# Router work of two MoE layers moved from behind the out projections to between their tiles

## The chip, the cores and the metric

One core of one Trainium2 chip runs the whole kernel. The metric is the device time of one launch in microseconds (us), median of the runs.

## The reference, cut to what matters

Two layers over 512 latent tokens and 256 context tokens of width 1024 (8 blocks of 128). In each layer a mixer writes `y`, and then a routed mixture of 16 experts follows. What the change touches:

```python
def modulate(x, g, shift, scale):
    return rms_norm(x, g) * (1 + scale) + shift
...
h = h + mod_l[2] * y_lat                       # out projection, gate, residual
h = h + mod_l[5] * expert_choice_ffn(modulate(h, ln2_g[layer], mod_l[3], mod_l[4]), *moe)
...
def expert_choice_ffn(h, w_router, w_gate, w_up, w_down):
    cap = max(1, EC_CAPACITY * t // N_EXPERTS)
    aff = jax.nn.softmax((h @ w_router).astype(F32), axis=-1)
    gate, idx = lax.top_k(jnp.swapaxes(aff, 1, 2), cap)
    xs = jax.vmap(lambda hb, ib: hb[ib])(h, idx)
    hid = jax.nn.silu(xs @ w_gate) * (xs @ w_up)
```

`cap` is 64 tokens of the latents and 32 of the context for each expert. Layer 0 routes both streams, layer 1 the latents alone.

## The kernel before, in words

Tokens lie in 6 tiles of 128 rows: tiles 0 and 1 are context, 2 to 5 latents. H holds the residual stream, one tile per 1024 columns. Each engine runs one written program, in order; an engine that waits on a semaphore runs nothing that stands behind the wait. There is no planner.

**Out projection.** Layer 0: `outproj0_pe` (L1781), tiles in the order YORDER = [0, 1, 4, 3, 5, 2], two halves of 512 columns each, so 12 halves j = 0 to 11. A half is 8 float32 products of 128x128 by 512 columns (L1789; the profile counts two records for a product). The first four halves have had 4 of their 8 products earlier. Layer 1: `outproj_pe` (L1812), 4 latent tiles, 8 halves (L1821). For each half DVE (`outproj_dve`, L1828) multiplies the result by the gate (L1838) and adds the half before it to H (L1846). PE may run four halves ahead (`op_ok`).

**Norm and router.** After the last half, ACT squares and sums each tile (L351; all but the last tile lie beside the projection), takes one root for all (L355), DVE inverts it (L371) and writes the normalised rows XM, tile by tile (L378). PE turns XM (L403: 48 transposes in layer 0, 32 in layer 1), DVE and ACT apply scale and shift per channel while copying out of PSUM to AM (L390, L364), and PE multiplies AM by the router weight in two parts (`logits_pe`, L1912; four blocks of channels side by side in 32-column groups). The four partial sums are copied (L1964, L1947), turned back (L1929) and added (L1974) into AFF. Then `pick_dve` (L1960): softmax from L1975 on, and the top tokens by eight rounds of max, index and replace (L1993 to L1996).

**Token lists and first pair.** The picks are turned (L1940), and DVE writes the lists TOKF, TOKL, TOKC, TOKX, TOKH (L2017 to L2031) and raises one semaphore, `sg`, at the last. POOL (`moe_pool`, L2323) then gathers rows of XM from memory: 128 latent rows for a pair of experts (L2328) and, in layer 0, 64 context rows (L2330); both raise `got`. PE waits for both, turns them (L2138, L2142) into banks 0, 1 and 4; DVE scales and shifts (L2244, 8 instructions, `xs` at the eighth), ACT the context rows (L2218, `xsc`). `pair` (L2167) waits for both and starts the expert products (L2104 latents, L2114 context).

**Queues.** SP's queue in `rows_sync` (L2043) stores H tiles (layer 0) as they are ready, issues seven 1 MB loads of expert rows after the first tile (`first_rows`, L2369), after the projection the rest of the first 8 (layer 1: 12) loads, and then stores all XM tiles. Later loads are released by PE slot by slot (L2367, `x_free`). POOL's queue loads the latents back to H (L2872, 2 MB), and in layer 0 the router weight WR only when the projection has ended (L2875, 64 KB); in layer 1 FING (L2879) and then WR (L2880) after the first half.

Of the kernel before, what the change touches and what calls it, by code (L numbers as in the profile page):

```python
# [12 lines left out]
P = 128  # L13
D = 1024
# [128 lines left out]
def build(nc, t, out):  # L143

    ctx = ExitStack()
    with ctx:
# [70 lines left out]
        dve_step, pool_step = sem("dve_step"), sem("pool_step")  # L217
# [104 lines left out]
        NORMS = ["n1_0", "n2_0", "n1_1", "n2_1"]  # L322
# [45 lines left out]
        def norm_dve(dve, n, tiles, xn, w, A, by_column=False, between=None, ready=None):  # L368
            runs, tiles0, ctx0 = before(n)
            dve.wait_ge(rt_ok, runs + 1)  # L370
            nc.vector.reciprocal(stat_t[:, 16 + tiles[0]:16 + NT], stat_t[:, 8 + tiles[0]:8 + NT]).then_inc(rc_ok, 1)  # L371
            dve.wait_ge(rc_ok, runs + 1)
            if n in ROUTED:
                nc.vector.memset(LG.rearrange("p t e -> p (t e)"), 0.0)
# [18 lines left out]
        def norm_pe(pe, n, tiles, xn, ctx_too):  # L393
            runs, tiles0, ctx0 = before(n)
            pe.wait_ge(xn_ok, tiles0 + len(tiles))
            for k in range(KT):
# [8 lines left out]
                if k == 5 and n in ROUTED:  # L405
                    logits_pe(pe, int(n[-1]), 0)
# [58 lines left out]
        for k in range(KT):  # L465
# [4 lines left out]
        g_mm, g_act, g_diff, g_ek, g_tr, g_rowT, g_rows = (sem(n) for n in (  # L470
            "g_mm", "g_act", "g_diff", "g_ek", "g_tr", "g_rowT", "g_rows"))
# [93 lines left out]
        def gates_rows_dve(dve):  # L565
            dve.wait_ge(g_tr, 1)
            nc.vector.tensor_copy(ROWT[0:32, 0:512], ps[0:32, 5, :])
            nc.vector.tensor_copy(ROWT[0:32, 512:768], ps[0:32, 6, 0:256]).then_inc(g_rowT, 1)
# [12 lines left out]
        def gates_exps_act(act):  # L581
# [3 lines left out]
            nc.scalar.activation(EK, GLAST, ACT.Exp).then_inc(g_ek, 1)  # L585
# [12 lines left out]
        def gates_rows_pe(pe):  # L598
# [5 lines left out]
            tr.then_inc(g_tr, 1)  # L604
# [223 lines left out]
        def gqa_act(act):  # L828
# [45 lines left out]
        cv_zero, cv_x, cv_c, cv_s, cv_tr, cv_outd, cv_outa, cv_xc = (sem(n) for n in (  # L874
            "cv_zero", "cv_x", "cv_c", "cv_s", "cv_tr", "cv_outd", "cv_outa", "cv_step"))
# [61 lines left out]
        def conv_dve(dve):  # L937
            step = Chain(dve, cv_xc)
# [73 lines left out]
        dn_qk, dn_zero, dn_step = (sem("dn_" + n) for n in "qk zero step".split())  # L1012
# [768 lines left out]
        def outproj0_pe(pe):  # L1781
# [23 lines left out]
            for j in range(2 * NT):  # L1805
                if j < 4:
                    half_products(j, range(4, KT))
                else:
                    pe.wait_ge(op_ok, j - 3)
                    half_products(j, turned + list(range(4, KT)))  # L1810

        def outproj_pe(pe, u0, tiles, ycols, mm_sem, ok_sem, base=0):  # L1812

            for j in range(2 * len(tiles)):
# [10 lines left out]
                if j < 2 * len(tiles) - 1:  # L1825
                    mm.then_inc(mm_sem, 1)

        def outproj_dve(dve, u0, tiles, mm_sem, prod_sem, ok_sem, w, PROD, base=0, banks=(4, 5, 6, 7)):  # L1828
            n = 2 * len(tiles)
            for j in range(n + 1):  # L1830
                if j < n:
                    tt, half = tiles[j // 2], j % 2
                    if j < n - 1:
                        dve.wait_ge(mm_sem, max(base - 1, 0) + j + 1)
                    else:
                        dve.wait_ge(w_free, u0 + KT)
                    v = 1 if tt < CT else 0
                    nc.vector.tensor_tensor(PROD[:, j % 4, :], ps[:, banks[j % 4], :], GATE[:, w, v, half * 512:half * 512 + 512],  # L1838
                                            ALU.mult).then_inc(ok_sem, 1)
                if j >= 1:  # L1840
                    tt, half = tiles[(j - 1) // 2], (j - 1) % 2
                    dve.wait_ge(ok_sem, base + j)
                    if w == 0 and base == 0:
                        dve.wait_ge(h_back if tt < CT else h_late, 16)
                    hh = H[:, tt, half * 512:half * 512 + 512]
                    nc.vector.tensor_tensor(hh, hh, PROD[:, (j - 1) % 4, :], ALU.add).then_inc(prod_sem, 1)  # L1846
# [5 lines left out]
        AM = region(6144, KT * AW, "p (k t) -> p k t", k=KT)  # L1852
# [30 lines left out]
        LT4 = region(13312, TOK, "p (t n) -> p t n", t=NT)  # L1883
        lg_ctx, lg_lat = sem("lg_ctx"), sem("lg_lat")
# [16 lines left out]
        def logits_pe(pe, l, half):  # L1901


            if half == 0:
                pe.wait_ge(mo["wr"], 16 * (l + 1))
            spans = [(4, LO, LAT)] + ([(5, 0, CTX)] if l == 0 else [])
            for bank, first, n in spans:
                for j in range(4):
                    k = 4 * half + j
                    w = WR[:, k, :]  # L1910
                    w = bass.AP(w.tensor, w.offset, [w.ap[0], [1, 32]])
                    mm = pe.matmul(ps[32 * j:32 * j + 32, bank, 0:n], w, AM[:, k, first:first + n],  # L1912
                                   start=(half == 0), stop=(half == 1))
            if half == 1:
                mm.then_inc(mo["lg"], 1)

        def pick_pe(pe, l):

            runs, _, ctx0 = before(NORMS[2 * l + 1])
            pe.wait_ge(am_ok, KT * (runs + 1))  # L1920
            if l == 0:
                pe.wait_ge(ac_ok, ctx0 + KT)
            logits_pe(pe, l, 1)
# [971 lines left out]
```

## Time and profile before

| | us |
|---|---|
| median of 3 runs | 2386.52 (2384.01 to 2393.23) |
| profiled execution, span first to last instruction | 2382.3 |
| PE busy in the span | 2112.3 (89%) |
| DVE busy | 762.8 (32%) |
| ACT busy | 447.2 (19%) |
| POOL busy | 121.9 (5%) |
| first out projection, from the end of its set-up | 749.4 to 818.1 |
| second out projection | 1794.1 to 1849.4 |

The page gives the profiled execution by its span alone; a time of its own around that span is not recorded, so the median stands beside it, 4.2 us longer. Times in the rows are in us from the span's start. L12 is line 12 of the kernel. PE is the matmul engine, DVE the vector engine, ACT the scalar engine, POOL GpSimd, SP the queue engine. PEclk is the granted clock of PE, 1.00 for 2.4 GHz and 0.50 for 1.2 GHz.

### The profile page before, as it was taken

Reading aid. Unit: us, or ns where it says so; the run is one execution under the profiler, and the core shown is the slowest. Engines: PE = TensorE matmul, PEld = TensorE weight load, DVE = VectorE, ACT = ScalarE, POOL = GpSimd, SP = SyncE. Lnnn points to the kernel's source line nnn. Section 1 sums busy time; section 2 is a strip of 40 time slices with the busy share of each in tenths; the row PEclk is TensorE's granted clock in tenths of the full one; section 3 lists DMA queues with packets and bytes.
Section 4 is the critical chain, followed back from the end, with each engine's and each line's share of the span. In section 5 each row is a group of like instructions: output and inputs, shape, how many; then the busy total and the mean of one; then the engine's idle time right before and its main releaser. Section 6 shows DMA issues by size and latency. Waiting matters only on the chain.

```text
span 2382.3 us, 32937 instructions
## 1 busy us (share of the span) xinstructions
PE 2112.3 (89%) x13760; PEld 1076.7 (45%) x13760; DVE 762.8 (32%) x1384; ACT 447.2 (19%) x1008; POOL 121.9 (5%) x119
## 2 busy tenths in 40 slices
PE   5998999818689849999999989999999399999997
PEld 3544666517685413333333334554674144444442
DVE  2143523588874341011011113000681511111113
ACT  2213421575321110000000012000561000000001
POOL 0000000030110000011111000000000000000000
PEclk9999999857679969999999999999999699999999
DMA  7219730132125339999999982210313399999996
GB/s 285 71 64 345 248 130 13 38 95 84 63 77 200 113 126 378 398 395 399 390 398 395 401 343 77 60 44 1 111 41 134 132 408 421 421 421 421 421 421 276
DMA packets 110618, 551.30 MB, mean 231 GB/s; under 512 B 13024, under 2 KB 25824, under 8 KB 61328
## 3 DMA queue, kind: packets, MB, share of 16 engines
q1 hardware_dynamic: 102512, 522.29, 55.6%
q0 software_dynamic: 7168, 23.83, 3.5%
q10 hardware_dynamic: 800, 3.15, 0.3%
q8 instruction: 111, 1.82, 0.3%
q14 instruction: 27, 0.22, 0.0%
HBM read 525.27 MB, written 22.38 MB: 230 GB/s over the span
## 4 chain that ended last, share of the span: by engine, by line
PE 75%; DMA 11%; DVE 9%; ACT 2%; issue 2%; SPq 0%; POOL 0%; DVEq 0%; POOLq 0%; ACTq 0%
PE ps L2104 22%; PE ps L2114 5%; DMA ring_sb<-expert_w_up 5%; PE ps L498 5%; PE ps L1789 3%; PE ps L901 3%; PE ps L2468 3%; PE ps L1821 2%; PE ps L2440 2%; PE ps L2449 2%; PE ps L2132 2%; DMA ring_sb<-ada_w 2%; PE ps L2151 2%; PE ps L900 2%; PE ps L244 2%
## 5 line engine op out<-in xcount | busy, mean ns | idle before, releaser
L2104 PE MATMUL ps<-work_sb 128*32 128x512 f32 (+1 forms) x2432 | 408.1, 593 | 9.6 <-ACT work_sb L2235 5.5
L2104 PE MATMUL ps<-ring_sb,work_sb 128*32 128x512 f32 (+1 forms) x2048 | 300.5, 599 | 16.6 <-DMA ring_sb<-expert_w_up 9.8
L2104 PEld LDWEIGHTS ps<-work_sb 128*32 128x32 f32 (+1 forms) x2432 | 123.0, 120 | 231.5 <-issue 224.2
L2104 PEld LDWEIGHTS ps<-ring_sb,work_sb 128*32 128x32 f32 (+1 forms) x2048 | 87.8, 118 | 204.3 <-issue 198.1
L2291 DVE TENSOR_TENSOR work_sb<-ps,work_sb 128x512 f32<-128x512 f32 x32 | 20.6, 687 | 437.1 <-PE ps L2114 329.8
L2225 ACT ACTIVATE work_sb<-ps 128x1024 f32<-128x1024 f32 x16 | 16.4, 1024 | 515.9 <-PE ps L2114 295.8
L498 PE MATMUL ps<-ring_sb,work_sb 128*128 128x512 f32 (+1 forms) x288 | 109.2, 541 | 0.9 <-DVE work_sb L390 0.9
L2114 PE MATMUL ps<-work_sb 128*32 128x512 f32 x768 | 100.7, 592 | 0.0
L2114 PE MATMUL ps<-ring_sb,work_sb 128*32 128x512 f32 x768 | 100.4, 593 | 0.0
L901 PE MATMUL ps<-work_sb,ring_sb 128*128 128x512 f32 x192 | 98.0, 592 | 0.0
L2310 DVE SCALAR_TENSOR_TENSOR work_sb<-ps,work_sb,gates_sb 128x1024 f32<-128x1024 f32 x16 | 20.5, 1284 | 232.9 <-PE ps L2114 124.8
L2235 ACT COPY work_sb<-ps 128x512 f32<-128x512 f32 x32 | 17.3, 589 | 405.7 <-PE ps L2192 405.7
L244 PE MATMUL ps<-ring_sb,sT_sb 128*32 128x512 f32 x384 | 57.0, 692 | 30.0 <-DMA ring_sb<-ada_w 28.2
L1789 PE MATMUL ps<-ring_sb,work_sb 128*128 128x512 f32 x192 | 82.8, 592 | 0.0
L498 PEld LDWEIGHTS ps<-ring_sb,work_sb 128*128 128x128 f32 x288 | 55.6, 194 | 52.4 <-issue 46.2
L2253 DVE TENSOR_TENSOR h_sb<-ps,h_sb 128x512 f32<-128x512 f32 x64 | 42.5, 688 | 100.2 <-PE ps L2151 100.2
L2468 PE MATMUL ps<-ring_sb,work_sb 128*128 128x512 f32 x160 | 68.8, 592 | 0.0
L2244 DVE TENSOR_SCALAR work_sb<-ps,scaleT_sb,modT_sb 128x128 f32<-128x128 f32 x128 | 42.2, 403 | 82.5 <-PE ps L2132 65.0
L2449 PE MATMUL ps<-work_sb,ring_sb 128*128 128x512 f32 x128 | 65.4, 592 | 0.0
L784 DVE TENSOR_REDUCE work_sb<-ps 128x1 f32<-128x768 f32 (+1 forms) x48 | 35.2, 775 | 78.5 <-PE ps L708 78.5
L2151 PE MATMUL ps<-work_sb 128*128 128x512 f32 x128 | 58.9, 604 | 1.5 <-DVE work_sb L2310 1.5
L2104 PE MATMUL ps<-h_sb,work_sb 128*64 128x512 f32 x128 | 57.6, 592 | 0.6 <-DMA work_sb<-expert_w_down 0.6
(405 smaller groups left out, 2913.2 us busy)
## 6 DMA issues: line engine op xcount, KB each, us to landing
work_sb<-expert_w_down SPq DMA_DIRECT2D x88, 1024.0 KB, 17.4
work_sb<-expert_w_gate SPq DMA_DIRECT2D x64, 1024.0 KB, 9.5
ring_sb<-expert_w_gate SPq DMA_DIRECT2D x64, 1024.0 KB, 10.0
ring_sb<-expert_w_up SPq DMA_DIRECT2D x64, 1024.0 KB, 13.9
work_sb<-expert_w_up SPq DMA_DIRECT2D x56, 1024.0 KB, 14.6
ring_sb<-ada_w SPq DMA_DIRECT2D x96, 512.0 KB, 6.2
ring_sb<-expert_w_down SPq DMA_DIRECT2D x32, 1024.0 KB, 14.4
ring_sb<-wout SPq DMA_DIRECT2D x16, 512.0 KB, 6.5
```

Source lines behind the costliest of these rows:

```text
L244: mm = pe.matmul(ps[32 * q:32 * q + 32, bank, :], sT[:, k, :], w[:, a * 512:(a + 1) * 512], start=(k == 0), stop=(k == KT - 1))
L498: mm = pe.matmul(ps[:, j % 4, 0:N], A[:, k, tok_cols(tt):tok_cols(tt) + P], w[:, (k % 2) * N:(k % 2 + 1) * N], start=(k == 0), stop=(k == ...
L900: pe.matmul(ps[:, b + 1, 0:CTX], w[:, k, :], A[:, k, 0:CTX], start=(k == 0), stop=(k == KT - 1))
L901: mm = pe.matmul(ps[:, b, :], w[:, k, :], A[:, k, LO:LO + LAT], start=(k == 0), stop=(k == KT - 1))
L1789: mm = pe.matmul(ps[:, EVEN_BANKS[j % 4], :], YT[:, tt, k, :], w[:, half * 512:half * 512 + 512], start=(k == 0), stop=(k == KT - 1))
L1821: mm = pe.matmul(ps[:, 4 + j % 4, :], c(k), w[:, half * 512:half * 512 + 512], start=(k == 0), stop=(k == KT - 1))
L2104: mm = pe.matmul(ps[g:g + wide, bank + n, :], lat_src[:, k, g:g + wide], us[e][:, n * 512:(n + 1) * 512], start=(k == 0), stop=(k == KT - 1))
L2114: mm = pe.matmul(ps[g:g + 32, bank_c, :], ctx_src(k, e), us[e][:, n * 512:(n + 1) * 512], start=(k == 0), stop=(k == KT - 1))
L2132: mm = pe.matmul(ps[:, k // 4, k % 4 * P:(k % 4 + 1) * P], XM[:, CT + j, cols(k)], TAKE[:, p % 2, j, :], start=(j == 0), stop=(j == LT - 1))
L2151: pe.matmul(ps[:, 4 + g % 4, :], ONEHOT[:, j * P:(j + 1) * P], YL[l][:, half * 512:half * 512 + 512], start=True, stop=True).then_inc(h_mm, 1)
L2449: mm = pe.matmul(ps[:, b, :], w[:, k, :], AO[:, k, LO:LO + LAT], start=(k == 0), stop=(k == KT - 1))
L2468: mm = pe.matmul(ps[:, 2 * (i % 2) + side, :], AO[:, k, v_cols(m):v_cols(m) + P], w, start=(k == 0), stop=(k == KT - 1))
```

## The change

The separate norm (`n2_0`, `n2_1`) and `logits_pe` go. The raw residual tile H is turned instead of the normalised one. The per-channel scale is multiplied into the router weight (WRM); the shift times the router weight becomes one row per stream (CROW, spread over the partitions as CVEC); the root of the mean square is applied to the logits. All of that is written between the halves of the out projection. PE:

```diff
+    def route_beside_pe(pe, l, j):        # called after the products of half j
+        if j == 1:
+            route_shift_pe(pe, l)         # waits for WR; 8 products, 16 columns
+        if j >= 4 and j % 2 == 0:
+            route_back_pe(pe, l, j // 2 - 2)
+        if j >= 2 and j % 2 == 0:
+            route_turn_pe(pe, l, j // 2 - 1)
+        if j == 3:
+            route_spread_pe(pe, l)
+        if j >= 3 and j % 2 == 1:
+            route_logits_pe(pe, l, (j - 3) // 2)
+    def route_end_pe(pe, l):              # after the last half
+        last = len(routed_tiles(l)) - 1
+        route_back_pe(pe, l, last - 1)
+        route_turn_pe(pe, l, last)
+        route_logits_pe(pe, l, last)
+        route_back_pe(pe, l, last)
+    def route_turn_pe(pe, l, n):
+        tt = routed_tiles(l)[n]
+        pe.wait_ge(op_x, OP0 * l + 2 * n + 2)
+        if n > 0:
+            pe.wait_ge(rt_dve, NT * l + n)
+            pe.wait_ge(rt_act, NT * l + n)
+        for k in range(KT):
+            tr = pe.transpose(ps[:, TURN_BANKS[l][k // 4], k % 4 * P:(k % 4 + 1) * P], H[:, tt, cols(k)], IDENT)
+            if k % 4 == 3:
+                tr.then_inc(rt_mm, 1)
+    def route_logits_pe(pe, l, n):
+        ...
+        for half in range(2):
+            pe.wait_ge((rt_dve, rt_act)[half], NT * l + n + 1)
+            for j in range(4):
+                k = 4 * half + j
+                ...
+                mm = pe.matmul(ps[32 * j:32 * j + 32, LOGIT_BANK[l], 0:P], w, RT[:, k, :], start=(half == 0), stop=(half == 1))
+        mm.then_inc(rl_mm, 1)
+    def route_back_pe(pe, l, n):
+        pe.wait_ge(rl_ok, logits_ok(l, 2 * n + 3))
+        pe.transpose(ps[:, BACK_BANK[l], 0:P], TURNED, IDENT).then_inc(rl_mm, 1)
```

DVE, the new body of `outproj_dve` for each half j, and what it calls:

```diff
+            for j in range(n):
+                ...
+                nc.vector.tensor_tensor(PROD[:, j % 4, :], ps[:, banks[j % 4], :], GATE..., ALU.mult).then_inc(ok_sem, 1)
+                dve.wait_ge(ok_sem, base + j + 1)
+                ...
+                nc.vector.tensor_tensor(hh, hh, PROD[:, j % 4, :], ALU.add).then_inc(prod_sem, 1)
+                if j == 2:
+                    router_weights_dve(dve, l)
+                if j % 2 == 0 and j >= 4:
+                    route_sums_dve(dve, l, j // 2 - 2)
+                if j % 2 == 1 and j >= 5:
+                    route_logits_dve(dve, l, (j - 5) // 2)
+                if j % 2 == 1 and j >= 3:
+                    route_dve(dve, l, (j - 3) // 2)
+            last = len(tiles) - 1
+            route_sums_dve(dve, l, last - 1)
+            route_dve(dve, l, last)
+            route_logits_dve(dve, l, last - 1)
+            route_sums_dve(dve, l, last)
+            route_logits_dve(dve, l, last)
+    def route_dve(dve, l, n):             # half of the turned tile, root, XM
+        ...
+        nc.vector.tensor_copy(RT[:, 0:4, :]..., ps[:, TURN_BANKS[l][0], :]).then_inc(rt_dve, 1)
+        dve.wait_ge(rt_ok, tile_roots_before(l) + n + 1)
+        nc.vector.reciprocal(...).then_inc(rc_ok, 1)
+        dve.wait_ge(rc_ok, tile_roots_before(l) + n + 1)
+        nc.vector.tensor_scalar(XM[:, tt, :], H[:, tt, :], stat_t[:, 16 + tt:17 + tt], None, ALU.mult).then_inc(xn_ok, 1)
+    def route_sums_dve(dve, l, n):
+        ...
+        nc.vector.tensor_copy(TURNED, ps[:, LOGIT_BANK[l], 0:P]).then_inc(rl_ok, 1)
+    def route_logits_dve(dve, l, n):
+        ...
+        nc.vector.tensor_reduce(LG[:, tt, :], groups, AX, ALU.add).then_inc(lg_ok, 1)
+        dve.wait_ge(lg_ok, NT * l + n + 1)
+        nc.vector.scalar_tensor_tensor(AFF[:, tt, :], LG[:, tt, :], ..., CVEC[...], ALU.mult, ALU.add).then_inc(rl_ok, 1)
```

ACT (`route_act`) squares each tile when both halves are in H, copies blocks 4 to 7 of the turned tile to RT (`rt_act`), and takes the root per tile. SP stores XM tile n - 1 behind H tile n and the last before the remaining expert loads. `router_weights_dve` forms WRM, copies CROW, and in layer 0 has the four memsets that stood in `pick_dve`. POOL's queue:

```diff
-            pool.wait_ge(gate_ok, 4)
-            pool.wait_ge(w_free, U_MOE[0])
+            pool.wait_ge(dn_ok, len(ORDER))
             pool.dma_start(WR, t["router"][0]...).then_inc(mo["wr"], 16)
...
             pool.wait_ge(op_mm, OP0)
+            pool.dma_start(WR, t["router"][1]...).then_inc(mo["wr"], 16)
             pool.dma_start(FING, ...).then_inc(fin_in, 16)
-            pool.dma_start(WR, t["router"][1]...).then_inc(mo["wr"], 16)
```

Token lists and first pair: TOKL is written first and raises `sg`, then TOKC raises it again (layer 0), the rest raises `sg_all`. The two gathers have semaphores of their own (`got`, `gotc`), and the latent rows of layer 0 are turned into banks 6 and 7.

```diff
-                pe.wait_ge(mp["got"], 32 * p + 32 if l == 0 else 32 * NPAIR + 16)
+                pe.wait_ge(mp["got"], 16 * (NPAIR * l + p + 1))
...
                 if l == 0:
+                    pe.wait_ge(mp["gotc"], 16 * p + 16)
...
+                    if m == 0 and k % 4 == 0:
+                        pe.wait_ge(mp["xs"], 2 * (NPAIR * l + p) + (k // 4 + 1 if l == 0 else 2))
...
+                        if m == 0 and k == 0:
+                            pe.wait_ge(mp["xsc"], p + 1)      # before the context products of block 0
```

Some semaphores elsewhere are merged (`g_tr` and `g_ek` into others, the convolution's chain into the common one) with the same instructions between them.

## Rows read from the trace of the kernel before

**Rows 1.** The page: chain shares by engine, and the group of the first out projection.

```profile
PE 75%; DMA 11%; DVE 9%; ACT 2%; issue 2%; SPq 0%; POOL 0%; DVEq 0%; POOLq 0%; ACTq 0%
...
L1789 PE MATMUL ps<-ring_sb,work_sb 128*128 128x512 f32 x192 | 82.8, 592 | 0.0
```

**Rows 2.** Chain of waits, in order of time, 720 to 900 us: start, us, what.

```profile
749.37 68.68 PE ps L1789 x160
...
818.69 1.71 DVE h_sb L1846 x2
...
841.20 0.27 DVE work_sb L1975
...
867.59 5.87 DMA work_sb<-xm_rows,work_sb
873.59 1.97 PE ps L2138 x8
875.59 2.65 DVE work_sb L2244 x8
...
879.31 3.64 PE ps L2104 x16
```

**Rows 3.** Chain of waits, 1848 to 1905 us.

```profile
1849.35 0.69 DVE work_sb L1838
...
1867.80 0.23 DVE work_sb L1975
```

**Rows 4.** Timeline of DVE, 720 to 815 us: start, us, engine, line, operation.

```profile
735.51 0.69 DVE L1751 TENSOR_TENSOR h_sb<-h_sb,work_sb 128x512 f32<-128x512 f32 x1
736.24 0.69 DVE L1752 TENSOR_TENSOR h_sb<-h_sb,work_sb 128x512 f32<-128x512 f32 x1
...
756.28 0.69 DVE L1838 TENSOR_TENSOR work_sb<-ps,gates_sb 128x512 f32<-128x512 f32 x1 [2.74 <-PE ps L1789]
756.89 0.68 DVE L1846 TENSOR_TENSOR h_sb<-h_sb,work_sb 128x512 f32<-128x512 f32 x1
```

**Rows 5.** Timeline, 63 us: a copy of 128 columns out of PSUM.

```profile
63.19 0.28 DVE L536 COPY work_sb<-ps 128x128 f32<-128x128 f32 x1
```

**Rows 6.** Timeline of PE: transposes, router logits, and 64-wide products.

```profile
747.46 1.91 PE L1761 MATMUL ps<-base_sb,h_sb 128*128 128x128 f32 x16
...
833.57 1.50 PE L1912 MATMUL ps<-work_sb 128*32 128x512 f32 x16
...
1787.97 1.09 PE L2540 MATMUL ps<-work_sb 128*64 128x128 f32 x16 [0.33 <-ACT work_sb L2621]
```

**Rows 7.** POOL's load of the latents; DMA issues, us to landing, 700 to 900 us.

```profile
749.68 0.78 POOL L2872 DMA_DIRECT2D h_sb<-x  x1 [18.16 <-PE ps L1761]
...
h_sb<-x POOLq DMA_DIRECT2D x1, 2048.0 KB, 8.7
...
work_sb<-router POOLq DMA_DIRECT2D x1, 64.0 KB, 2.2
```

**Rows 8.** Token lists: first and last of DVE, POOL's first gather and its landing.

```profile
863.64 0.15 DVE L2017 TENSOR_SCALAR work_sb<-ps 64x1 f32<-64x1 f32 x1 [0.54 <-PE ps L1941]
...
865.25 0.17 DVE L2031 TENSOR_SCALAR work_sb<-ps 64x16 uint32<-64x16 f32 x1
...
866.25 1.04 POOL L2328 DMA_INDIRECT work_sb<-xm_rows,work_sb  x1 [44.05 <-DVE work_sb L2031]
...
DMA to landing us min/median/max: 5.0/5.0/5.0
```

**Rows 9.** Stretches: busy us (x) per engine, PEclk, DMA share, GB/s.

```profile
820.00:822.00 2.00, 0.00 (x0) 0.00 (x0) 0.39 (x1) 1.45 (x3) 1.88 (x3) 0.91 0.44 170
828.00:830.00 2.00, 2.00 (x11) 1.90 (x10) 1.58 (x2) 1.13 (x2) 0.00 (x0) 0.50 1.04 438
832.00:834.00 2.00, 1.91 (x15) 1.32 (x17) 1.73 (x3) 1.24 (x3) 0.00 (x0) 1.00 0.99 262
...
1792.00:1796.00 4.00, 2.27 (x13) 1.07 (x9) 1.02 (x1) 2.07 (x3) 0.00 (x0) 1.00 0.01 2
```

More of the change, by code:

```diff
@@ L1010, in attn @@
             return ATB[:, i % 2, h, :]
-        dn_qk, dn_zero, dn_step = (sem("dn_" + n) for n in "qk zero step".split())
+        dn_qk, dn_zero = sem("dn_qk"), sem("dn_zero")
         dn_grow, dn_spill = ([sem(f"dn_{n}{b}") for b in range(4)] for n in ("grow", "spill"))
@@ L1826, in outproj_pe, with outproj_dve @@
                     mm.then_inc(mm_sem, 1)
-        def outproj_dve(dve, u0, tiles, mm_sem, prod_sem, ok_sem, w, PROD, base=0, banks=(4, 5, 6, 7)):
+                route_beside_pe(pe, 1, j)
+            route_end_pe(pe, 1)
+        def outproj_dve(dve, l, u0, mm_sem, prod_sem, ok_sem, PROD, banks=(4, 5, 6, 7)):
+            tiles, base = routed_tiles(l), OP0 * l
             n = 2 * len(tiles)
[L1830 to L1846, printed above, removed]
@@ new lines, in build, with routed_tiles @@
+        CVEC = region(30912, 2 * NE, "p (v e) -> p v e", v=2)
+        TURNED = region(30944, P)
+        CROW = region(31072, NE)[0:2, :]
+        TURN_BANKS, LOGIT_BANK, BACK_BANK = ((1, 3), (0, 1)), (7, 2), (4, 3)
+        def routed_tiles(l):
+            return YORDER if l == 0 else list(range(CT, NT))
+        def route_turn_pe(pe, l, n):
[8 more added lines that the diff above has]
+                    tr.then_inc(rt_mm, 1)
@@ new lines, in route_shift_pe, with route_spread_pe @@
+        def route_shift_pe(pe, l):
+            if l == 0:
+                pe.wait_ge(yt_ok, NT)
+            pe.wait_ge(mo["wr"], 16 * (l + 1))
+            pe.wait_ge(modT_ok, MODULATED["n2_%d" % l])
+            for k in range(KT):
+                mm = pe.matmul(ps[0:2, LOGIT_BANK[l], P:P + NE], modT[:, :, 3, k], WR[:, k, :], start=(k == 0), stop=(k == KT - 1))
+            mm.then_inc(rl_mm, 1)
+        def route_spread_pe(pe, l):
+            pe.wait_ge(rl_ok, logits_ok(l, 1))
+            for v in range(2):
+                mm = pe.matmul(ps[:, BACK_BANK[l], P + v * NE:P + (v + 1) * NE], bc(IDENT[0:2, v:v + 1], [2, P]), CROW,
+                               start=True, stop=True)
+            mm.then_inc(rl_mm, 1)
@@ new lines, in router_weights_dve @@
+        def router_weights_dve(dve, l):
+            dve.wait_ge(mo["wr"], 16 * (l + 1))
+            nc.vector.memset(CVEC.rearrange("p v e -> p (v e)"), 0.0)
+            for v in range(2):
+                nc.vector.tensor_tensor(WRM[:, v], WR, bc(AT[:, 1, v, :].unsqueeze(2), [P, KT, NE]), ALU.mult)
+            dve.wait_ge(rl_mm, logits_mm(l, 1))
+            nc.vector.tensor_copy(CROW, ps[0:2, LOGIT_BANK[l], P:P + NE]).then_inc(rl_ok, 1)
+            if l == 0:
+                rows = C0 + NE
+                nc.vector.memset(ROWS0[0:rows, :], -1.0)
+                nc.vector.memset(TOPS[0:rows, :], 0.0)
+                nc.vector.memset(PICKF[0:rows, :], 0.0)
+                nc.vector.memset(AFFC[:, :, 0:C0], 0.0)
@@ L1899, in tiles_of @@
             return range(NT) if l == 0 else range(CT, NT)
[L1901 to L1915, printed above, removed]
-        def pick_pe(pe, l):
[L1919 to L1923, printed above, removed]
-            for i, tt in enumerate(tiles_of(l)):
-                if tt == 0:
-                    pe.wait_ge(lg_ctx, 1)
-                elif tt == CT:
-                    pe.wait_ge(lg_lat, l + 1)
-                tr = pe.transpose(ps[:, 6 + tt // 4, tt % 4 * P:tt % 4 * P + P], LT4[:, tt, :], IDENT)
-            tr.then_inc(mo["lg"], 1)
+        def pick_pe(pe, l):
             pe.wait_ge(mo["aff"], l + 1)
@@ L2670, in odd_dve @@
             oatt_dve(dve, step)
-            outproj_dve(dve, U_OUT1, list(range(CT, NT)), op_mm, op_x, op_ok, 0, OPROD, OP0)
-            dve.wait_ge(op_x, OP0 + 2 * LT)
+            outproj_dve(dve, 1, U_OUT1, op_mm, op_x, op_ok, OPROD)
         def odd_act(act):
```

184 lines of the change are left out of this document (113 added, 71 removed).

## The prediction

> **What bounds the kernel now.** I read the page's chain shares first: PE is 75% of the path that sets the end and DMA 11% [rows 1], so whatever lengthens PE's queue counts in full unless PE was waiting there. Then I read the chain of waits around the two places that the change touches. In layer 0 the out projection runs on PE without a gap until 818.05 (749.37 + 68.68) [rows 2]. From there to the softmax's first step at 841.20 the path goes through adds, norm, transposes and logits: 23.15 us in which PE mostly waits. In layer 1 the same stretch runs from 1849.35 to 1867.80, 18.45 us [rows 3]. The softmax and the eight rounds of picking behind it don't change. Behind those comes the start of the first pair, 863.6 to 879.31 in layer 0 [rows 2, 8]. So the change can win in two stretches of about 23 and 18 us and at the starts. The stretch in front of them, where it puts the work, is PE-bound: a record of L1789 takes 0.592 us and starts every 0.43 (82.8 / 192) [rows 1], so a half costs 16 x 0.43 = 6.87 us with nothing idle. Any wait put there is paid.
>
> **The price list.** DVE: an operation over 512 columns takes 0.69; one that depends on it starts 0.73 after it did (735.51 to 736.24), one that doesn't 0.61 after (756.28 to 756.89) [rows 4]. A copy of 128 columns out of PSUM takes 0.28 [rows 5]. The reduce of 64 and the small product behind it I take at 0.26 and 0.10, by the 0.27 of a larger small one [rows 2]; bounds 0.1 and 0.3 each. PE: transposes cost 1.91 / 16 = 0.12 each in a row [rows 6], the 8 of a tile 0.9 and a single one 0.1. The logits of a tile are 16 records of 128 columns in four column groups. From below, a quarter of the 1.50 us that 16 records with up to 512 columns took gives 0.4; from above, 16 records of 128 columns in two groups took 1.09 [rows 6]. I take 0.6, nearer the row with the same weight width. The shift's products (16 columns) I take at 0.6 too, bounds 0.3 and 1.1. A semaphore costs some 0.05.
>
> **Where the new waits are.** Let D be the moment a half's last product ends and DVE's multiply starts; PE could have gone on at D - 0.16 (0.592 - 0.43). The order written out decides the rest. Behind half j PE next needs something that DVE makes only after the multiply and add of that same half:
> - j = 3: multiply D, add D + 0.73, copy to RT D + 1.34 to 2.03, PE at D + 2.07. The stall is 2.2, the logits 0.6; the spread of CROW hides in the stall. 2.8.
> - even j from 4: the turned-back logits need TURNED, copied D + 1.34 to 1.62, so PE goes on at D + 1.66. Stall 1.8, one transpose 0.1, turn of the next tile 0.9. 2.8.
> - odd j from 5: reduce D + 1.34, small product D + 1.60, copy to RT D + 1.70 to 2.39, PE at D + 2.43. Stall 2.6, logits 0.6. 3.2.
> Queued behind the waiting instruction are the next half's products, and nobody fills the hole. That RT could have been copied a whole half earlier (the turn was done at the end of half j - 1) doesn't help, since DVE stands before the multiply. ACT's copy, squares and roots lie beside the products; what hides them is 6.87 us per half, of which they take under 2.
>
> **Layer 0, projection.** j = 1 waits for the router weight. POOL's queue issues it behind the 2 MB of latents, issued at 749.68 and landed 8.7 later at 758.4; alone it lands in 2.2 [rows 7]. If it went past, it would be there at 753 and cost nothing; if it started only afterwards, at 760.6. I take just behind, 758.7, because it shares the queue. PE would be ready at 749.37 + 6.87 - 0.16 = about 756.1, so 2.6 lost (bounds 0 and 4.5), then the shift's 0.6. Turn of the first tile after j = 2: 0.9. j = 3: 2.8. j = 4, 6, 8, 10: 11.2. j = 5, 7, 9: 9.6. Together 27.7, so D of the last half is 845.8 instead of 818.05.
>
> **The tail behind the last half**, counted from its D: RT copy until 2.4; logits of tile 4 2.5 to 3.3; its TURNED copy until 3.65 (DVE scales XM in between); PE turns it back and then the last tile, 3.7 to 4.9; DVE's and ACT's copies until 5.1 and 5.5; last logits 5.6 to 6.4; root, inverse and the last XM until 6.8, reduce and product of tile 4 until 7.1; TURNED 7.35; back 7.7; reduce and product, softmax at 8.2. Against 23.15 this saves 14.95. The router of layer 0 is thus 27.7 - 14.95 = 12.8 later than before.
>
> **Layer 1.** The weight is issued first after half 0 and, by the 2.2 of its landing, is there before half 1 ends; the queue's other load FING is needed only at the end. Shift 0.6, turn 0.9, j = 3 2.8, j = 4 and 6 5.6, j = 5 3.2: 13.1. The tail is the same 8.2 against 18.45, saving 10.25. 2.9 later.
>
> **The starts.** The first list now precedes the other small writes: two writes from 863.64 end at about 863.9 instead of 865.42, so POOL's first gather, 866.25 before, goes out 1.5 earlier, its landing 5.0 later at 869.7 [rows 8]; the second lands 1.5 earlier at 871.9 (867.59 + 5.87 - 1.5). PE turns the latents 869.8 to 871.7 while the second is in flight (1.97 for 8 [rows 2]), DVE scales four blocks at 0.33 by 873.2, PE turns the context rows meanwhile, and the first product can begin at 873.25 instead of 879.31: 6.1 saved. The context products of block 0 need ACT's scaling, which shifts with its transposes by 3.6 to 875.7; 8 latent products at the low clock (3.64 [rows 2]) cover that. PE is also busier before the products, so the clock may return sooner; I give it 0.7, bounds 0 and 2. In layer 1 PE waits for both halves of `xs`, so only the list's 0.4 is won. Later pairs gain nothing: their tokens are turned a whole product ahead. The expert loads are released by PE's progress and shift with it; the XM stores, now earlier, have the 25 us of picking as cover. The merged semaphores cost nothing.
>
> The row of the transposes bears on that 0.7: the clock stood at 0.50 in 828 to 830 and at 1.00 in 832 to 834, and of PE's work from 826.35 on only transposes had run before it rose [rows 9]. The Trainium skill (TensorE: Matmul & The Clock Gate, Part 4: PE-mode transpose) says that transposes don't count as activity for the clock. By that the 0.7 would be 0; the trace of this case says otherwise, and I go by it.
>
> **The sum.** +12.8 + 2.9 - 6.1 - 0.7 - 0.4 = +8.5. The profiled execution would span 2382.3 + 8.5 = 2390.8; against the median of the runs, 2386.5, that is 2395.0. At most 0.3 off in each of the 12 stalls is 3.6, the router weight -2.6 to +1.9, eight groups of logits and shift -2.8 to +4, the two tails 1.5 each. They won't all lean one way: about 5.5 either side, 2389.5 to 2401.
>
> **The rivals.**
> - *The waits don't bite* (the DVE work is done before PE asks). Then the 12 stalls, 2.2 + 4 x 1.8 + 3 x 2.6 in layer 0 and 2.2 + 2 x 1.8 + 2.6 in layer 1, 25.6 in all, vanish: 2395.0 - 25.6 = 2369.4. For it speaks only that DVE is busy 32%; against it the written order. 6 in 100. That the change doesn't do what it says is part of it: the order is plain in the diff, so no more.
> - *The clock falls in the projections* (slower side). PE now stands idle 1.8 to 2.6 us in each half. A stretch with 1.73 idle in 4 stayed at 1.00; after the end at 818.05 the clock had begun to fall in 820 to 822 (0.91) [rows 9]. Gaps of 2.6 lie between these. It decides if an idle of some 2.6 is enough. Halves at 1.2 GHz take 6.87 more; 8 in layer 0 and 4 in layer 1 are 82 us, half of them slow makes +41: 2436. 7 in 100. The Trainium skill (same page, A second HAM failure mode: psum-queue depth-cycling) tells of a kernel whose frequent short idles made the clock swing, which is this rival.
> - *Both gathers land together*, so the split gives little: XG turned from 871.9, four blocks scaled at 875.3, 4.0 saved instead of 6.8: 2397.8. For it speaks that they share a queue and start 1.3 apart, against it the landing of 5.0 measured for the first alone [rows 8]. 12 in 100, half of it over the line.
>
> **How the numbers follow.** The forecast holds 75 in 100. About 0.5% (12 us) is what a measurement can tell from no change; slower by that begins at 2398.4. Of the forecast's own spread a quarter lies above it, 18; with 7 from the clock and 6 from the gathers that is 0.31. Faster is the first rival, 0.06. Within 0.5% remains 0.63. The range takes the bounds and the gathers and leaves out the clock and the vanished stalls: 2387 to 2405.
>
> **What would show it.** In the profile after: the records of L1789's successor no longer follow each other; before each logits product an idle PE of 2 to 2.6 released by the DVE copy to RT, before each turn one of 1.8 released by the copy to TURNED, and one of 2 to 3 in front of the shift released by the router's DMA; the last half of layer 0 ends 27 us later, and the softmax follows within 8 to 9; PEclk 1.00 in both projections; the first expert product starts 9.5 to 10 after the first list instead of 15.7. It would be wrong if those idles are shorter than 1 us, if PEclk falls between halves, or if the tail takes over 12.

## The result and the profile after

| | median, us (range, runs) | profiled span |
|---|---|---|
| before, same chip | 2387.06 (2384.01 to 2393.23, 4 runs) | 2382.3 |
| after | 2406.26 (2396.81 to 2413.69, 4 runs) | 2411.9 |

The ratio is 1.0086, interval [1.0057, 1.0114]: slower by 19.2 us, where +8.5 was forecast. The sign was right, the size was not, and 2406.3 lies above the range's 2405, by 1.3. The interval lies wholly above 1.005, so the case "within 0.5%", to which the forecast gave 0.63, did not come. The profiled execution of the changed kernel was the slowest of its four (2413.69), so the difference of the two spans, 29.6, overstates what the change costs.

The first reading is whether the waits are where the written order puts them. PE's timeline of the changed kernel, layer 0's projection, columns start, duration, engine, line, operation, and in brackets the idle time before it with what ended it:

```profile
749.69 7.03 PE L1793 MATMUL ps<-ring_sb,work_sb 128*128 128x512 f32 x16
758.98 0.55 PE L1900 MATMUL ps<-work_sb,modT_sb 128*2 128x16 f32 x16 [2.25 <-issue]
759.46 5.40 PE L1793 MATMUL ps<-ring_sb,work_sb 128*128 128x512 f32 x8
...
765.64 3.60 PE L1793 MATMUL ps<-ring_sb,work_sb 128*128 128x512 f32 x8
769.17 0.61 PE L1907 MATMUL ps<-work_sb,base_sb 2*128 2x16 f32 x4
771.35 0.64 PE L1922 MATMUL ps<-work_sb 128*32 128x128 f32 x16 [1.57 <-DVE work_sb L1994]
771.92 7.13 PE L1793 MATMUL ps<-ring_sb,work_sb 128*128 128x512 f32 x16
780.87 0.33 PE L1928 MATMUL ps<-base_sb,work_sb 128*128 128x128 f32 x1 [1.81 <-DVE work_sb L2005]
781.03 1.13 PE L1889 MATMUL ps<-base_sb,h_sb 128*128 128x128 f32 x8
782.00 7.03 PE L1793 MATMUL ps<-ring_sb,work_sb 128*128 128x512 f32 x16
791.64 0.64 PE L1922 MATMUL ps<-work_sb 128*32 128x128 f32 x16 [2.61 <-DVE work_sb L1994]
792.22 7.13 PE L1793 MATMUL ps<-ring_sb,work_sb 128*128 128x512 f32 x16
...
832.03 1.08 PE L1922 MATMUL ps<-work_sb 128*32 128x128 f32 x16 [2.61 <-DVE work_sb L1994]
833.04 8.09 PE L1793 MATMUL ps<-ring_sb,work_sb 128*128 128x512 f32 x16
```

They are: 2.61 in front of the logits behind each odd half from j = 5, 1.7 to 1.8 in front of the turn back behind each even half from j = 4, 1.57 plus the 0.61 of the spread behind j = 3, and 2.25 in front of the shift. Logits (0.57 from start to next start) and shift (0.48) cost about the 0.6 that was forecast, and the spread hides in its stall as forecast. Two rows don't fit: the 8 records from 759.46 take 5.40 where the next 8 take 3.60, and the half at 833.04 takes 8.09 where the others take 7.03 or 7.13. The logits ahead of it, too, take 1.08 for 0.64.

DVE's timeline of the changed kernel behind one even and one odd half shows who holds PE: multiply, add, (reduce, small product,) copy.

```profile
779.10 0.69 DVE L1846 TENSOR_TENSOR work_sb<-ps,gates_sb 128x512 f32<-128x512 f32 x1 [6.94 <-PE ps L1793]
...
780.53 0.28 DVE L2005 COPY work_sb<-ps 128x128 f32<-128x128 f32 x1
789.07 0.69 DVE L1846 TENSOR_TENSOR work_sb<-ps,gates_sb 128x512 f32<-128x512 f32 x1 [8.26 <-PE ps L1793]
789.80 0.69 DVE L1852 TENSOR_TENSOR h_sb<-h_sb,work_sb 128x512 f32<-128x512 f32 x1
790.41 0.22 DVE L2012 TENSOR_REDUCE work_sb<-ps 128x16 f32<-128x64 f32 x1
...
790.81 0.68 DVE L1994 COPY work_sb<-ps 128x512 f32<-128x512 f32 x1
```

DVE had been idle for 6.94 and 8.26 us before these multiplies, and the data of both copies had been in PSUM for nearly all of that time (logits from 771.35, turned tile from 781.03). This answers to [rows 4, 5]: the steps have the durations of before.

The router weight in POOL's timeline of the changed kernel:

```profile
750.16 0.78 POOL L3008 DMA_DIRECT2D h_sb<-x  x1 [20.84 <-PE ps L1765]
750.93 0.56 POOL L3010 DMA_DIRECT2D work_sb<-router  x1
```

And in its DMA issues of 745 to 765 (operation, count, KB each, us from issue to landing):

```profile
h_sb<-x POOLq DMA_DIRECT2D x1, 2048.0 KB, 8.5
...
work_sb<-router POOLq DMA_DIRECT2D x1, 64.0 KB, 8.0
```

Issued at 750.93 and landed 8.0 later, at 758.9: forecast 758.7. The same 64 KB took 2.2 alone [rows 7]. Layer 1 shows that the order of issue matters: in the kernel before, the router weight issued 0.6 behind the 512 KB of FING landed 3.6 after its issue, 0.3 behind FING; in the changed kernel, issued ahead of FING, it took 2.1.

PEclk answers to [rows 9]. Windows of the changed kernel (stretch, length, PE, PEld, DVE, ACT, POOL busy, clock, DMA share, GB/s):

```profile
759.00:763.00 4.00, 4.00 (x21) 2.04 (x22) 0.00 (x0) 0.36 (x2) 0.00 (x0) 0.61 1.02 332
...
771.00:779.00 8.00, 7.65 (x32) 3.33 (x32) 1.12 (x3) 0.88 (x2) 0.00 (x0) 1.00 0.36 143
831.00:833.00 2.00, 0.97 (x16) 0.66 (x16) 1.68 (x5) 1.06 (x2) 0.00 (x0) 0.65 0.64 262
833.00:837.00 4.00, 4.00 (x11) 1.84 (x8) 0.00 (x0) 0.00 (x0) 0.00 (x0) 0.75 0.33 131
```

Both odd rows are the clock: 0.61 in 759 to 763, 0.65 and 0.75 in 831 to 837, 1.00 between (771 to 779). So it did fall inside the projection, which the prediction had put at 7 in 100, but for a few us at a time and not for half of it. "If PEclk falls between halves" was one of the prediction's own signs of being wrong.

The tail and the start of the first pair, chain of waits of the changed kernel (answers to [rows 2, 8]):

```profile
851.05 0.70 DVE work_sb L1846
...
859.23 0.24 DVE work_sb L2012
...
859.76 0.27 DVE work_sb L2100
...
881.73 0.34 PE ps L2078
...
883.38 4.67 DMA work_sb<-xm_rows,work_sb
...
888.19 1.97 PE ps L2279 x8
890.19 1.38 DVE work_sb L2383 x4
891.61 3.62 PE ps L2243 x13
```

From the last multiply (851.05) to the softmax (859.76) 8.71, for 23.1 before. From the turned picks (881.73) to the first expert product (891.61) 9.88, for 16.15; only the gather of the latent rows stands in it, and the product follows the fourth scaled block.

### The profile page after: what moved, and what is told of

Read it like the earlier page. It is cut to its first block, busy times and chain, and to the rows that moved or that the text cites. A ratio compares the mean times of both kernels' runs of the same rounds, so it can differ in the third digit from the quotient of the medians.

```text
span 2411.9 us, 33299 instructions
## 1 busy us (share of the span) xinstructions
PE 2127.1 (88%) x13912; PEld 1082.9 (45%) x13912; DVE 766.3 (32%) x1420; ACT 449.5 (19%) x1017; POOL 120.1 (5%) x119
## 4 chain that ended last, share of the span: by engine, by line
PE 75%; DMA 11%; DVE 9%; ACT 3%; issue 1%; SPq 0%; POOL 0%; DVEq 0%; POOLq 0%; ACTq 0%
PE ps L2243 22%; DMA ring_sb<-expert_w_up 6%; PE ps L2255 5%; PE ps L503 4%; PE ps L1793 4%; PE ps L906 3%; PE ps L2612 3%; PE ps L1827 2%; PE ps L2584 2%; PE ps L2593 2%; DMA work_sb<-expert_w_up 2%; PE ps L2273 2%; DMA ring_sb<-ada_w 2%; PE ps L2293 2%; PE ps L905 2%; PE ps L244 2%
## 5 line engine op out<-in xcount | busy, mean ns | idle before, releaser
L1793 PE MATMUL ps<-ring_sb,work_sb 128*128 128x512 f32 x192 | 89.4, 621 | 0.0
L244 PE MATMUL ps<-ring_sb,sT_sb 128*32 128x512 f32 x384 | 56.3, 682 | 28.1 <-DMA ring_sb<-ada_w 26.8
L2612 PE MATMUL ps<-ring_sb,work_sb 128*128 128x512 f32 x160 | 68.8, 592 | 0.0
L1827 PE MATMUL ps<-ring_sb,work_sb 128*128 128x512 f32 x128 | 57.7, 606 | 1.7 <-DVE work_sb L2732 1.7
## 6 DMA issues: line engine op xcount, KB each, us to landing
ring_sb<-expert_w_gate SPq DMA_DIRECT2D x64, 1024.0 KB, 10.7
ring_sb<-expert_w_up SPq DMA_DIRECT2D x64, 1024.0 KB, 16.2
```

The source lines that it names most:

```text
L244: mm = pe.matmul(ps[32 * q:32 * q + 32, bank, :], sT[:, k, :], w[:, a * 512:(a + 1) * 512], start=(k == 0), stop=(k == KT - 1))
L1793: mm = pe.matmul(ps[:, EVEN_BANKS[j % 4], :], YT[:, tt, k, :], w[:, half * 512:half * 512 + 512], start=(k == 0), stop=(k == KT - 1))
L1827: mm = pe.matmul(ps[:, 4 + j % 4, :], c(k), w[:, half * 512:half * 512 + 512], start=(k == 0), stop=(k == KT - 1))
L2612: mm = pe.matmul(ps[:, 2 * (i % 2) + side, :], AO[:, k, v_cols(m):v_cols(m) + P], w, start=(k == 0), stop=(k == KT - 1))
```

## The experiments

All kernels run both layers in full. "hoisted" means that a copy was put ahead of DVE's wait for a half.

To compare kernels beyond the 0.5% of a timing, I cut each profile into stages between the same instructions: first projection (from the context turn at L1765 of the changed kernel to the last half's multiply), its tail (to the softmax), picking, start (to the first expert product), and the same for layer 1, whose projection I count from its first product. Worked out from the timelines, in us (2nd and 3rd are further profiles of the same kernel):

```
                    proj0   tail0  pick0  start0  proj1  tail1  pick1  start1    sum
before              70.62   23.12  21.96  16.15   55.23  18.45  20.12  11.06   236.7
before, 2nd         70.61   22.85  21.31  15.63   55.24  18.74  19.85  11.01   235.2
after              103.11    8.71  21.97   9.88   71.04   8.27  20.28  10.75   254.0
after, 2nd         101.85    9.73  21.96   9.99   70.89   8.61  20.27  10.70   254.0
after, 3rd         102.87    8.27  21.95  10.19   70.88   8.62  20.27  10.78   253.8
weight early        99.30    8.27  21.95  10.24   69.39   8.27  20.27  10.61   248.3
RT copy hoisted     93.50    8.04  21.96   9.81   65.08   8.12  20.28  10.69   237.5
both hoisted        84.11    8.48  21.95   9.79   61.09   8.11  20.27  10.70   224.5
both, weight early  80.14    7.93  21.96  10.37   61.09   7.73  20.27  10.73   220.2
same, 2nd           80.15    7.95  21.96  10.34   61.09   8.03  20.27  10.76   220.6
starts only         70.62   23.06  21.96  10.19   55.23  18.44  20.09  10.64   230.2
longer waits       108.69   10.34  21.95   9.72   75.14  10.34  20.27  10.72   267.2
```

### The changed kernel again

No edit, timed again beside the kernels below.

> The changed kernel once more, nothing edited. The theory that the layer-0 expert stage of the first profile was slow by chance (its pairs took 66.1 to 70.5 us against 66.1 to 67.9 before, PE waiting about 16 us for expert rows against 8) expects a median of 2395 to 2403 and a profile whose seven pair periods sum to 469 to 473 us. The rival, that the change makes that stage slower, expects the sum at 478 to 483 us again and a time of 2404 or more. Both expect the 12 idles of 1.6 to 2.8 us in the projections.

Measured 2406.5 (2395.8 to 2412.2, 7 runs) against 2384.94 for the kernel before (23 runs): 1.0079 [1.0047, 1.0111]. The loss stands. The stages differ by 18.0 on the mean of three profiles against two; that is 0.75%, which is all of the ratio within its interval. The first theory, an expert stage slow by chance and a median of 2395 to 2403, missed: the median is where the rival put it, and the pair periods of this profile sum to 477.1, between the two. More on that stage further down.

### Both copies hoisted

```diff
 for j in range(n):
+    if j % 2 == 0 and j >= 4:
+        route_sums_dve(dve, l, j // 2 - 2)      # TURNED
+    if j % 2 == 1 and j >= 3:
+        turned_dve(dve, l, (j - 3) // 2)        # RT, taken out of route_dve
     if j < n - 1:
         dve.wait_ge(mm_sem, max(base - 1, 0) + j + 1)
...
-    if j % 2 == 0 and j >= 4:
-        route_sums_dve(dve, l, j // 2 - 2)
```

> DVE copies the turned tile to RT, and the logits to TURNED, ahead of the multiply of the half in front of which PE asks for them, not behind its add. Nothing else is edited. The theory of the 12 waits expects them gone: some 26 us less than the changed kernel (first projection 70.6 + about 11 us long up to its last product, second 55 + 5), up to 5 us more if the fallen clock goes with them; so 2370 to 2380, faster than the kernel before by 0.3 to 0.7%. The rival, that PE work put between the halves is itself the price, expects less than 5 us.

Measured 2373.46 (2368.7 to 2377.0, 10 runs), 0.9957 [0.9939, 0.9975]. PE's timeline of this kernel:

```profile
765.61 7.13 PE L1793 MATMUL ps<-ring_sb,work_sb 128*128 128x512 f32 x16
772.58 0.27 PE L1931 MATMUL ps<-base_sb,work_sb 128*128 128x128 f32 x1
...
773.64 7.03 PE L1793 MATMUL ps<-ring_sb,work_sb 128*128 128x512 f32 x16
780.60 0.64 PE L1925 MATMUL ps<-work_sb 128*32 128x128 f32 x16
781.18 7.13 PE L1793 MATMUL ps<-ring_sb,work_sb 128*128 128x512 f32 x16
```

No idle of PE is left in these rows, and the time lies in the expected 2370 to 2380. The same router work goes on, and a pair of halves takes 15.57 (765.61 to 781.18) where it took 20.30 (771.92 to 792.22). So what makes the difference is the position of two copies in DVE's order; the router's products are the same in both.

### Both hoisted, and the router weight early

```diff
+    pool.wait_ge(dn_ok, len(ORDER))
+    pool.dma_start(WR, t["router"][0]...).then_inc(mo["wr"], 16)
     pool.wait_ge(yt_tr, NT)
     pool.dma_start(H[:, CT:NT, :], ...)
-    pool.wait_ge(dn_ok, len(ORDER))
-    pool.dma_start(WR, t["router"][0]...).then_inc(mo["wr"], 16)
```

> As hoist_both, and the router weight of layer 0 is issued on POOL's queue ahead of the 2 MB of latents, not behind them. The theory expects the idle of 2.25 us in front of the shift's products to go: 2.4 us less than hoist_both, 4 if the low clock behind it goes too. The rival, that the weight lands early anyway and PE waits there for something else, expects no difference.

Its wait goes ahead with it, and so the weight is issued at 727.35, 16 us before the latents, and lands in 2.1.

Measured 2362.72 (2362.3 to 2363.4, 5 runs), 0.9911 [0.9883, 0.9939]. PE's timeline of this kernel:

```profile
743.07 7.03 PE L1793 MATMUL ps<-ring_sb,work_sb 128*128 128x512 f32 x16
750.03 0.55 PE L1903 MATMUL ps<-work_sb,modT_sb 128*2 128x16 f32 x16
750.52 3.70 PE L1793 MATMUL ps<-ring_sb,work_sb 128*128 128x512 f32 x8
```

The first projection is 4.0 shorter than with the copies alone (84.11 to 80.14). The wait was 2.2; the other 1.7 is the 8 records behind it, 3.70 in place of 5.40. The medians fell by 10.7, which is more than the 4 that the edit explains; the second timing of this version, below, is 7.5 longer. What the router's products cost where nothing waits is 80.14 - 70.62 = 9.5 in layer 0 and 61.09 - 55.23 = 5.9 in layer 1.

### Only the starts

The kernel before, with the token lists, gathers and halves of XG from the change, and its merged semaphores, and nothing else (L2017 to L2031, L2138 to L2142, L2167, L2244, L2323 on of its text).

> The kernel before with the start part of the change alone: token list first, gathers with semaphores of their own, tokens scaled in halves, banks 6 and 7 for the latents of layer 0; norm and router as before. The theory expects the first expert product of layer 0 6.3 us sooner after the picks are turned (9.9 instead of 16.2), 0.3 sooner in layer 1, the expert stage itself unchanged (pair periods summing to 469 to 472 us), and so 2379 to 2381. The rival, that the halves or the banks make the expert stage of layer 0 slower, expects the sum at 478 or more and a time of 2388 or more.

Measured 2377.6 (2373.4 to 2387.2, 10 runs), 0.9976 [0.9954, 0.9998]. POOL's timeline of this kernel:

```profile
859.50 1.03 POOL L2336 DMA_INDIRECT work_sb<-xm_rows,work_sb  x1 [42.57 <-DVE work_sb L2018]
```

PE's timeline of the same stretch:

```profile
864.61 1.96 PE L2147 MATMUL ps<-base_sb,work_sb 128*128 128x128 f32 x8 [6.32 <-DMA work_sb<-xm_rows,work_sb]
868.03 3.18 PE L2111 MATMUL ps<-ring_sb,work_sb 128*32 128x512 f32 x16 [0.31 <-DVE work_sb L2251]
```

The latent rows land 5.1 after their issue and PE turns them (864.61) without waiting for the context rows. 10.19 from the picks to the product against 15.6 to 16.2: this part is worth 5.7 in the profile and 7.3 in the medians.

### One part at a time: the weight early, or only RT hoisted

The same edits as above, each alone on the changed kernel.

> The changed kernel with one edit: the router weight of layer 0 issued ahead of the latents on POOL's queue; the 12 waits stay. Adding up by stages expects 4.1 us less than the changed kernel (2.4 for the idle in front of the shift, 1.7 for the low clock of the half behind it), about 2402, with the layer-0 expert stage as slow as in the two profiles of the changed kernel (923 to 926 us up to the second out projection). The rival, that this idle at the start is what also slows the expert stage (the weight edit gave 10.7 on top of the reordered kernel), expects 2396 or less and that stage at 915 to 917.

> Only the copy of the turned tile to RT is moved ahead of the multiply; the copy to TURNED stays behind the add. By the waits of the profile (1.6 + 0.6 at j = 3 and 2.6 + 0.16 at each odd j from 5, six of the twelve in both layers) the theory expects 15 us less than the changed kernel: 2390 to 2393; the six waits of 1.7 to 1.8 in front of the transpose stay. The rival, that the fallen clock and not the waits made most of the loss, expects the second half of the saving (to 2373) to come as well.

The weight early: 2398.51 (9 runs), 1.0064 [1.0041, 1.0087]; its first projection is 3.3 below the changed kernel's mean (102.6 to 99.3), where 4.1 was expected: one slow half stands in it (8.30), 1.6, and 0.9 in the mean of the three. The second, which the edit doesn't touch, is 1.5 shorter: in this profile no half of it is a slow one, all take 7.03 or 7.13, so 1.5 is a fall's price there. RT hoisted: 2386.59 (10 runs; 2390 to 2393 was expected), 1.0022 [1.0004, 1.0041]; 9.1 and 5.9 less in the projections, by 4 and 2 waits gone (2.2 + 3 x 2.6 = 10.0 and 2.2 + 2.6 = 4.8). The waits for TURNED stay, and in this profile the clock fell behind one of them:

```profile
778.08 0.33 PE L1931 MATMUL ps<-base_sb,work_sb 128*128 128x128 f32 x1 [1.81 <-DVE work_sb L2009]
...
779.22 8.73 PE L1793 MATMUL ps<-ring_sb,work_sb 128*128 128x512 f32 x16
```

Neither part alone pays for the change. The two together weren't run; by the stages they would come to 237.5 - 4.0 = 233.5 for some 236 before, an estimate, and only with the waits for TURNED gone, too, was a kernel measured clearly ahead.

### Before and after, once more

> The kernel before once more, for its stages: the span up to the transposes in the first out projection (747.5 us in the first profile, 741 to 748 in the other kernels, in which nothing up to there differs in work) and the layer-0 expert stage (914.8). If these vary by chance, they come out anywhere in 741 to 748 and 912 to 920; the projections, tails and starts must repeat within 0.3 us (70.6, 23.1, 16.2; 55.2, 18.5, 11.1).

> The changed kernel a third time, for the layer-0 expert stage. Chance expects it in 912 to 920 us this time; the rival, that the changed kernel makes it slower, expects 922 to 926 a third time, with PE's waits for expert rows at 14 us or more there.

One profiled execution each: 2380.98 and 2409.71. The first profile of the changed kernel had layer 0's expert stage and second mixer (first expert product to second out projection) at 925.8 for 914.8 before, which had looked like a second loss, and the second profile had 922.8. The new ones give 916.7 for before and 916.3 for after. So the same program takes 916 or 926 there, and the change doesn't make that stage slow each time. The rival of the early weight, that the idle in front of the shift slows it, falls too: the kernels with RT alone or both copies hoisted have that idle and take 915.8 and 915.2.

Whether it is all chance isn't settled. Of the four profiles with all twelve waits in place three are long (925.8, 922.8, and 920.6 with the longer waits below), of the eight others none (914.6 to 917.0). Two of the long ones come from the slowest of 4 and of 7 executions (2413.69, 2412.24), and the medians leave 1 to 4 us for all that stands outside the stages of the table.

The stages of before repeat within 0.3 as expected, but for the first start (15.63 for 16.15) and the first picking, on which nothing had been staked (21.31 for 21.96).

### Longer waits

A reduce over 512 columns whose result nobody uses, ahead of every copy to RT. It lengthens the odd waits by 0.6 and changes nothing else.

```diff
+nc.vector.tensor_reduce(MX[:, 3, 0:1], ps[:, TURN_BANKS[l][0], :], AX, ALU.add)
 nc.vector.tensor_copy(RT[:, 0:4, :]..., ps[:, TURN_BANKS[l][0], :]).then_inc(rt_dve, 1)
```

> The changed kernel with one useless DVE sum over 512 columns ahead of each copy to RT, so that each of the waits in front of the logits is 0.6 us longer (3.2 instead of 2.6; 10 of them, one each in the tails among them). If a wait costs only its length: 6 us more than the changed kernel, about 2411, with one to three falls of the clock in the projections as before. The rival, that a wait of 3.2 lets the clock fall where one of 2.6 seldom does, expects up to 1.7 more for each of the 6 waits in front of another half: about 2421, and halves of 8 us and more behind most logits.

Measured 2420.31 (4 runs), 1.0131 [1.0101, 1.0161]. PE's timeline of this kernel:

```profile
811.30 0.65 PE L1922 MATMUL ps<-work_sb 128*32 128x128 f32 x16 [3.20 <-DVE work_sb L1995]
811.87 8.83 PE L1793 MATMUL ps<-ring_sb,work_sb 128*128 128x512 f32 x16
...
833.79 1.08 PE L1922 MATMUL ps<-work_sb 128*32 128x128 f32 x16 [3.21 <-DVE work_sb L1995]
834.80 9.66 PE L1793 MATMUL ps<-ring_sb,work_sb 128*128 128x512 f32 x16
```

The window over the second of these halves, columns as above (clock 0.67):

```profile
834.00:843.00 9.00, 9.00 (x29) 3.94 (x22) 0.50 (x1) 0.00 (x0) 0.00 (x0) 0.67 0.16 66
```

Length alone is four waits of 0.6 in the first projection, two in the second, and two copies in each tail: 2.4 + 1.2 + 2.4 = 6.0. The stages grew by 267.2 - 253.9 = 13.3, of which 6.1 and 4.2 in the projections. The surplus of 3.7 and 3.0 is slow halves: 8.83 and 9.66 for 7.13, and in the second projection 8.83 (behind j = 3, whose wait grew from 1.57 to 2.17) and 9.55. Three of the four waits of 3.2 inside the projections were followed by a slow half, for 5 of 12 of the waits of 2.61. The medians agree: 1.0131 against 1.0079 is 12 us, and 2420 is what the rival expected. So a longer idle costs more than its length, and the clock is the surplus. It is one profile, though, and a longer wait also moves all that follows it to another time, which wasn't held fixed.

### The best version again

> The kernel with both copies ahead of the multiply and the early router weight once more, as the version to keep. The sum of its stages (first projection 80.1, tail 7.9, start 10.4, second projection 61.1, tail 7.7, start 10.7) must repeat within 0.5 us each; the time must be 2362 to 2372, at least 0.4% faster than the kernel before. If the steadiness of its five runs (2362.3 to 2363.4) was chance, the runs spread over some 8 us this time.

Measured 2370.25 (2366.4 to 2374.1, 5 runs), 0.9929 [0.9904, 0.9953]. Its stages repeat within 0.1 in all but the second tail (0.3); the medians of the two timings differ by 7.5 with nothing in the kernel changed, so the narrow spread of the first five runs was chance. The version beats the kernel before by 0.7 to 0.9%.

## Why the prediction was wrong, though its mechanism was right

**The mechanism was right.** "DVE stands before the multiply" is what costs the time: taking the 8 waits of layer 0 away gave 99.30 - 80.14 = 19.2, of which some 1.6 is the one slow half (8.30) in the profile with the waits, so about 17.5 for the forecast 2.2 + 7.2 + 7.8 = 17.2; layer 1, between two profiles without a slow half, gave 69.39 - 61.09 = 8.3 for 8.4. The router weight came 0.2 later than forecast. The gathers did not land together.

Term by term, mean of three profiles after less mean of two before, forecast in brackets: first projection +32.0 (27.7), its tail -14.1 (-14.95), start -5.9 (-6.8), second projection +15.7 (13.1), tail -10.1 (-10.25), start -0.3 (-0.4), picking +0.3 twice (0). Together +18.0 for +8.5 (8.4 by the rounded terms). The medians say 19.2 and 21.6; the rest is no larger than the scatter of the stages that the change doesn't touch.

**The step that failed is the clock term of the projections, which the sum put at nothing.** It took every half at 6.87, full clock, and gave a falling clock only the form of a rival that holds for half the time, 2436 at 7 in 100. The runs show short falls worth 4.1 us in the two projections. Of the 9.5 missing, 6.9 lie in the two projections:
- Always a fall behind the router-weight wait: 5.40 for 3.70, in every profile that has that wait and in none that hasn't. 1.7.
- One more in layer 0 in each profile, behind a wait of 2.61: inside the projection in two (halves of 8.09 and 8.05; 1.4 and 1.3 with their logits), in front of the tail in the second (logits of 1.08, tail 9.73). One in the second projection in all three (8.36, 8.19, 8.18; 1.5 to 1.6 with their logits). In the projections that is 0.9 and 1.5 in the mean of the three.
- No clock, but waits and turns a little longer than in the sum, the second term that was too small. The stretch from 771.92 to 782.00 takes 10.08 and the one from 792.22 to 802.20 9.98, for 6.87 + 2.8; the one from 782.00 to 792.22 takes 10.22, for 6.87 + 3.2. Six even ones at 0.3 to 0.4 and four odd ones at 0.15 are 2.6. D lies 0.1 later behind logits, PE goes on some 0.15 later behind the turned copy, and a turn of 8 transposes takes 0.97 for 0.9.

The other 2.6 are the tails, 1.0 (at the low clock in part: 8 transposes take 1.42 for 1.13 in the first profile, logits 1.08 for 0.64 in the second), the starts, 1.0, and the picking, 0.6.

The rival and the forecast were set up as an either-or, "it decides if an idle of some 2.6 is enough", with a price for half the halves. The records show a third case: the clock falls behind some idles, stays low for about half a half, and costs 1.3 to 1.7 each time. In the three profiles of the changed kernel that was 8 of 39 waits inside the projections, and 4.1 us per run (1.7 + 0.9 + 1.5), a term of the sum and not a rival. With it and the 2.6 above the forecast would have been 2402.

**The 0.7 for a sooner clock was not there.** The first records of the expert products, in PE's timeline of the changed kernel:

```profile
891.61 3.64 PE L2243 MATMUL ps<-ring_sb,work_sb 128*32 128x512 f32 x16
```

That is 3.64 as before [rows 2]; it was 3.18 in the kernel with only the starts, 0.5 sooner. The Trainium skill (TensorE: Matmul & The Clock Gate, Part 4: PE-mode transpose) gave 0 here, and the changed kernel agrees with it; the rows of before, where the clock rose behind nothing but transposes [rows 9], still don't. What raises it there wasn't tried by itself.

**What stays open.** Why the clock falls behind some waits and not behind others of the same 2.61. The Trainium skill (same page, A second HAM failure mode: psum-queue depth-cycling) tells of short idles that make the clock swing; the runs agree in kind, with those 8 falls behind 39 idles. Also, from the first pair's first activation on ACT to the second's, the first expert pair of layer 1 took 54.7 and 56.3 in the two profiles of before, 56.3 in the first of after, and 57.9 or 58.0 in the other two, in steps of 1.6 to 1.7 that go with a low clock. A window inside that pair, the second profile of after, clock 0.66:

```profile
1940.00:1950.00 10.00, 10.00 (x48) 5.98 (x48) 2.26 (x6) 1.02 (x1) 0.00 (x0) 0.66 1.01 422
```

The like window of the kernel before, first profile, clock 1.00:

```profile
1910.00:1920.00 10.00, 10.00 (x64) 5.60 (x62) 0.91 (x2) 1.02 (x1) 0.00 (x0) 1.00 1.02 430
```

The change isn't needed for it: the kernel with only the starts, whose projections are those of before, took 57.9 too, and so did four more profiles of edited kernels. Whether the change makes it likelier is not settled; it is at most 3 us.

## What to carry to other kernels

Work put into the gaps of a stage that PE bounds costs more than its own products when what it needs stands in another engine's order behind that stage's own step: here 9.5 us of router products became 32, and moving two copies ahead of a wait gave 28 us back in the two projections. Before such a change, write for each new wait what the releasing engine does first, and ask whether the data were there earlier. And give every new idle of PE a second term, the clock that it may lose, instead of asking only whether the clock falls for good.

## What was not expected of the hardware

- A short fall of the clock has nearly one price: 1.7 behind the idle of 1.81 (8.73 for 7.03), 1.7 behind 2.25 (5.40 for 3.70 in 8 records) and 1.3 to 1.6 behind 2.6 (logits 0.44 and half 0.9 to 1.2 more). Behind 3.2 a half lost up to 2.5 and its logits 0.44.
- The idle of 2.2 before the shift let the clock fall in all six profiles that have it, those of 2.61 in front of the logits in one of three (6 of 18 in the three profiles of the changed kernel; in 3 more, all in tails, it fell a microsecond or two later), those of 1.7 to 1.8 once in 36. What follows differs, 16 records of 16 columns in the first case and of 128 in the second, and so does what goes before; these runs don't separate them.
- A 64 KB load issued 0.8 us behind a 2 MB one on POOL's queue landed 8.0 after its issue, just behind the large one, where alone it took 2.2; behind 512 KB it took 3.6, ahead of them 2.1. That was forecast; not forecast was that its 2.2 us wait cost 4.0 in all.
